# Wide moving operand in the convolutional stage, mLSTM decay rows on the free row half, and a reordered opening of the feed-forward stages

## The reference

```python
def swiglu(h, w_gu, w_down):                 # four times
    g, u = jnp.split(h @ w_gu, 2, axis=-1)
    return (jax.nn.silu(g) * u) @ w_down

# mLSTM scores of the mixer of the first stack, 8 heads of 64: exp(decay terms) * (q @ k.T)

def conv_gated_ffn(x, w_up, conv_w, conv_b, w_down):      # twice
    h = x @ w_up                              # 1024 -> 2 * 2816
    h = causal_depthwise_conv(h, conv_w, width=3) + conv_b
    gate, val = jnp.split(h, 2, axis=-1)
    return (jax.nn.silu(gate) * val) @ w_down
```

## Time and profile before

| | |
|---|---|
| time, three runs | 1957.45 us median (1957.35 to 1958.13) |
| the profiled execution | 1958.44 us, its span 1955.8 us |
| PE busy | 1941.7 us (99%), 11580 matmuls |
| PEld busy | 1706.1 us (87%) |
| DVE busy | 1269.5 us (65%) |
| ACT busy | 1099.4 us (56%) |
| DMA | 335.82 MB, mean 172 GB/s |

### The profile page before, as it was taken

How to read it: one execution, slowest core, us unless ns; L and a number is a source line. 1 busy time by engine, 2 the same in 40 slices (tenths; PEclk the granted TensorE clock), 3 DMA queues, 4 the chain that set the end, 5 groups by cost and what they waited for, 6 DMA issues and landing times.

```text
span 1955.8 us, 29401 instructions
## 1 busy us (share of the span) xinstructions
PE 1941.7 (99%) x11580; PEld 1706.1 (87%) x11580; DVE 1269.5 (65%) x2141; ACT 1099.4 (56%) x1717; POOL 6.5 (0%) x18
## 2 busy tenths in 40 slices
PE   9999999999999999999999999999999999999998
PEld 7888899999788888888989988888989998989997
DVE  5555777466655575557865676556758777758775
ACT  5444666554644564456774655446656556646554
POOL 0000000000000000000000000000000000000000
PEclk9999999999999999999999999999999999999999
DMA  8656445546566556645454546664536555536562
GB/s 278 192 184 184 161 132 171 162 131 197 187 190 186 172 184 193 185 156 175 134 179 152 155 158 217 188 184 146 166 108 205 181 186 165 160 114 199 179 187 82
DMA packets 93688, 335.82 MB, mean 172 GB/s; under 512 B 10224, under 2 KB 12528, under 8 KB 93552
## 3 DMA queue, kind: packets, MB, share of 16 engines
q1 hardware_dynamic: 92112, 328.51, 54.0%
q0 software_dynamic: 720, 4.37, 0.6%
q10 hardware_dynamic: 720, 1.07, 0.2%
HBM read 332.86 MB, written 1.05 MB: 171 GB/s over the span
## 4 chain that ended last, share of the span: by engine, by line
PE 94%; DVE 4%; ACT 1%; DMA 1%; issue 1%; DVEq 0%; ACTq 0%
PE stream L1797 11%; PE stream L1798 10%; PE stream L1799 10%; PE stream L1803 10%; PE stream L1805 10%; PE stream L1804 10%; PE acc L1803 8%; PE acc L1805 8%; PE acc L1804 8%; PE stream L1897 1%; DVE w_lo L1061 1%; PE acc L2208 1%; PE acc L2006 1%; DMA w_raw<-in_w_down 1%; PE stream L2203 0%
## 5 line engine op out<-in xcount | busy, mean ns | idle before, releaser
L1061 DVE TENSOR_TENSOR w_lo<-w_raw,w_hi 128x1024 fp32r<-128x1024 f32 x624 | 759.7, 1223 | 391.4 <-ACT w_hi L550 390.4
L550 ACT ACTIVATE w_hi<-w_raw 128x1024 fp32r<-128x1024 f32 x624 | 655.1, 1055 | 423.4 <-PE stream L1805 208.6
L1797 PE MATMUL stream<-h_hi,w_hi 128*128 128x256 f32 x1440 | 417.0, 290 | 1.1 <-DVE conv_tiles L1513 0.9
L1798 PE MATMUL stream<-h_lo,w_hi 128*128 128x256 f32 x1440 | 407.0, 283 | 0.0
L1799 PE MATMUL stream<-h_hi,w_lo 128*128 128x256 f32 x1440 | 407.0, 283 | 0.0
L1803 PE MATMUL stream<-w_hi,h_hi 128*128 128x512 f32 x896 | 353.9, 395 | 0.0
L1805 PE MATMUL stream<-w_lo,h_hi 128*128 128x512 f32 x896 | 349.2, 390 | 0.0
L1804 PE MATMUL stream<-w_hi,h_lo 128*128 128x512 f32 x896 | 348.8, 389 | 0.0
L1797 PEld LDWEIGHTS stream<-h_hi,w_hi 128*128 128x128 f32 x1440 | 275.4, 191 | 6.4 <-issue 2.4
L1798 PEld LDWEIGHTS stream<-h_lo,w_hi 128*128 128x128 f32 x1440 | 275.7, 191 | 0.9
L1799 PEld LDWEIGHTS stream<-h_hi,w_lo 128*128 128x128 f32 x1440 | 275.3, 191 | 0.0
(11 more groups left out here) (312 smaller groups left out, 2183.3 us busy)
## 6 DMA issues: line engine op xcount, KB each, us to landing
w_raw<-in_w_up SPq DMA_DIRECT2D x264, 512.0 KB, 3.7
w_raw<-in_w_mix SPq DMA_DIRECT2D x228, 512.0 KB, 3.6
w_raw<-in_w_down SPq DMA_DIRECT2D x132, 512.0 KB, 3.7
params<-in_params POOLq DMA_DIRECT2D x4, 859.5 KB, 5.7
out_x<-x_residual SPq DMA_DIRECT2D x4, 256.0 KB, 2.4
constants<-in_consts POOLq DMA_DIRECT2D x1, 832.0 KB, 7.6
x_residual<-in_x ACTq DMA_DIRECT2D x3, 256.0 KB, 7.1
x_residual<-in_x SPq DMA_DIRECT2D x1, 256.0 KB, 3.6
```

Source lines behind the costliest of these rows:

```text
L550: nc.scalar.activation(w_hi[:, u % RING], w_raw[:, u % RAW], ACT.Copy).then_inc(hi_ready, 1)
L1061: nc.vector.tensor_tensor(w_lo[:, u % RING], w_raw[:, u % RAW], w_hi[:, u % RING].bitcast(F32), ALU.subtract).then_inc(split_done, 1)
L1797: nc.tensor.matmul(dst, w_hi[:, s, w], hi, start=first, stop=False)
L1798: nc.tensor.matmul(dst, w_hi[:, s, w], lo, start=False, stop=False)
```

## The change

- The convolutional stage: h_hi and h_lo become two halves of one tile h_both. A k-block is now one matmul with 512 moving columns, [h_hi | h_lo], against w_hi, and one with 256 columns, h_hi, against w_lo. A bank then holds two partial sums side by side. For i > 1 ACT copies the second half to a new tile c_sum (semaphore conv_part), DVE adds the first half to it (semaphore conv_in), and the convolution reads c_sum. PE takes a bank again when the sum of i-2 is made, not when its convolution is done (i = 3 is as before).
- The mLSTM scores: the decay rows and the row selector also lie in partitions 64 to 127; a head reads them from the half that its q and k do not use, and the five matmuls alternate.
- The opening of `ffn`: one of the five splits ahead of the root moves behind the rounding of chunk 0, on ACT and on DVE.

```diff
         mo_tok, _ = sb("out_gate_tok", [P, QT, D], at=h32_at)
-        h_hi, _ = sb("h_hi", [P, KT, T], F32R)
-        h_lo, _ = sb("h_lo", [P, KT, T], F32R)
+        h_both, _ = sb("h_both", [P, KT, 2 * T], F32R)
+        h_hi, h_lo = h_both[:, :, 0:T], h_both[:, :, T:2 * T]
         cst, _ = sb("constants", [P, NC])
...
-        sel_r, _ = sb("row_select", [64, HEADS], F32R)
+        sel_r, _ = sb("row_select", [P, HEADS], F32R)
...
-        nm, _ = sb("neg_m_rows", [64, T], F32R)
+        nm, _ = sb("neg_m_rows", [P, T], F32R)
...
+        c_sum, _ = sb("conv_sums", [P, 4, T])
...
         def conv_tile(i, side_i):
-            return (side[side_i] if i == 0 else bank[2 * (i % 2) + side_i])[:, 0:T]
+            return (side[side_i] if i == 0 else bank[2 * (i % 2) + side_i])[:]
+
+        def conv_src(i, side_i):
+            return conv_tile(i, side_i)[:, 0:T] if i < 2 else c_sum[:, 2 * (i % 2) + side_i]
 
...
 
-                for j in range(5):
+                for j in range(4):
                     hi_next()
...
                 chunk_round(0)
+                hi_next()
                 hi_next()
...
                     for side_i in range(2):
+                        if i > 1:
+                            act.wait_ge(unit_done, u0 + up2_at(i, side_i) + 1)
+                            act.wait_ge(conv2_done, 2 * n + side_i - 3)
+                            nc.scalar.activation(c_sum[:, 2 * (i % 2) + side_i], conv_tile(i, side_i)[:, T:2 * T],
+                                                 ACT.Copy).then_inc(conv_part, 1)
                         if 2 * i + side_i >= 3:
...
                         else:
-                            act.wait_ge(unit_done, u0 + up2_at(i, side_i) + 1)
+                            act.wait_ge(conv_in, 2 * (l * (NF - 2) + i - 2) + side_i + 1)
                         if n > 1:
                             act.wait_ge(gated, n - 1)
-                        nc.scalar.activation(cbuf[:, 2 * (i % 2) + side_i], conv_tile(i, side_i), ACT.Identity,
+                        nc.scalar.activation(cbuf[:, 2 * (i % 2) + side_i], conv_src(i, side_i), ACT.Identity,
                                              scale=p2("conv_w", (2 * 2 + side_i) * NF + i),
...
 
-                for j in range(5):
+                for j in range(4):
                     lo_next()
...
                 chunk_rest(0)
+                lo_next()
                 lo_next()
...
                                                     ALU.mult)
-                        nc.vector.tensor_tensor(sel_r[:], ident[0:64, 0:HEADS], ident[0:64, 32:32 + HEADS],
-                                                ALU.add)
+                        for b in (0, 64):
+                            nc.vector.tensor_tensor(sel_r[b:b + 64], ident[b:b + 64, b:b + HEADS],
+                                                    ident[b:b + 64, b + 32:b + 32 + HEADS], ALU.add)
                     nc.vector.tensor_tensor(lamp[:, 0:1], p1("lam", 0), p1("lam", 1), ALU.mult)
...
                     dve.wait_ge(nm_cleared, l + 1)
-                    nc.vector.tensor_copy(nm[0:HEADS], neg_m[:]).then_inc(rows_split, 1)
-                    dve.wait_ge(rows_split, l * 2 + 1)
-                    nc.vector.tensor_tensor(nm[32:32 + HEADS], neg_m[:], nm[0:HEADS].bitcast(F32),
-                                            ALU.subtract).then_inc(rows_split, 1)
+                    for b in (0, 64):
+                        nc.vector.tensor_copy(nm[b:b + HEADS], neg_m[:]).then_inc(rows_split, 1)
+                    dve.wait_ge(rows_split, l * 4 + 2)
+                    for b in (32, 96):
+                        nc.vector.tensor_tensor(nm[b:b + HEADS], neg_m[:], nm[0:HEADS].bitcast(F32),
+                                                ALU.subtract).then_inc(rows_split, 1)
 
...
                         s = 2 * (i % 2) + side_i
+                        if i > 1:
+                            dve.wait_ge(conv_part, 2 * (l * (NF - 2) + i - 2) + side_i + 1)
+                            nc.vector.tensor_tensor(c_sum[:, s], conv_tile(i, side_i)[:, 0:T], c_sum[:, s],
+                                                    ALU.add).then_inc(conv_in, 1)
                         if 2 * i + side_i >= 3:
...
                             r = nc.vector.scalar_tensor_tensor(
-                                out=cbuf[:, s, back:], in0=conv_tile(i, side_i)[:, 0:T - back],
+                                out=cbuf[:, s, back:], in0=conv_src(i, side_i)[:, 0:T - back],
                                 scalar=p2("conv_w", ((2 - back) * 2 + side_i) * NF + i),
...
                         pe.wait_ge(qk_silu, l + 1)
-                        pe.wait_ge(rows_split, l * 2 + 2)
+                        pe.wait_ge(rows_split, l * 4 + 4)
                         pe.wait_ge(sc_masked, (n8 + HEADS) * 2)
...
                     q, k = y[r, h // 2], y[r, 4 + h // 2]
-                    row = sel_r[:, h:h + 1].to_broadcast([64, P])
+                    z = slice(64 - 64 * (h % 2), 128 - 64 * (h % 2))
+                    row = sel_r[z, h:h + 1].to_broadcast([64, P])
                     nc.tensor.matmul(side[1][:, 0:3 * P], ident_r[:], neg_r[:], start=True, stop=False)
-                    nc.tensor.matmul(side[1][:, 0:T], row, nm[:], start=False, stop=False)
-                    nc.tensor.matmul(side[1][:, T:3 * P], row, nm[:, P:T], start=False,
-                                     stop=True).then_inc(mlstm_sc, 1)
                     nc.tensor.matmul(side[0][:, 0:T], k[:, 0:P], q, start=True, stop=True)
+                    nc.tensor.matmul(side[1][:, 0:T], row, nm[z], start=False, stop=False)
                     nc.tensor.matmul(side[0][:, T:3 * P], k[:, P:T], q[:, P:T], start=True,
                                      stop=True).then_inc(mlstm_qk, 1)
+                    nc.tensor.matmul(side[1][:, T:3 * P], row, nm[z, P:T], start=False,
+                                     stop=True).then_inc(mlstm_sc, 1)
 
...
                             pe.wait_ge(open_taken, l * 2 + side_i + 1)
+                        elif i == 3:
+                            pe.wait_ge(conv2_done, 2 * (l * NF + i - 2) + side_i + 1)
                         else:
-                            pe.wait_ge(conv2_done, 2 * (l * NF + i - 2) + side_i + 1)
-                        model_unit(conv_tile(i, side_i), u, h_hi, h_lo,
-                                   (lambda k: turn_open(1) if k == 4 else None) if (i, side_i) == (2, 0) else None)
+                            pe.wait_ge(conv_in, 2 * (l * (NF - 2) + i - 4) + side_i + 1)
+                        dst = conv_tile(i, side_i)
+                        for k in range(KT):
+                            if k == 4 and (i, side_i) == (2, 0):
+                                turn_open(1)
+                            w = slice(k * P, (k + 1) * P)
+                            nc.tensor.matmul(dst, w_hi[:, u % RING, w], h_both[:, k], start=(k == 0), stop=False)
+                            r = nc.tensor.matmul(dst[:, 0:T], w_lo[:, u % RING, w], h_hi[:, k], start=False,
+                                                 stop=(k == KT - 1))
+                        r.then_inc(unit_done, 1)
                     if i >= LAG:
```

More of the change, by code:

```diff
@@ L390, in build @@
         ln_stat = sem("ln_stat")
+        conv_in = sem("conv_in")
+        conv_part = sem("conv_part")
         open_out = sem("open_out")
```

## The result

The changed kernel takes 1947.81 us (median of 5 runs, 1947.64 to 1948.49) against 1957.45 us of the kernel before (5 runs, 1957.24 to 1958.69): 9.6 us less, a ratio of 0.995 with a 95% interval of 0.9939 to 0.9961. 1946.0 was predicted. In the profiled executions the span goes from 1955.8 to 1946.0 us, 9.8 less.

The account below looks back on a forecast made before the run. PE was taken to bound the kernel, with 94% of the chain. Convolutional part 6.0 + mLSTM scores 3.4 + opening 2.0 = 11.4 us less than 1957.45 us gave 1946 us; forecast range 1943 to 1950 us, chance 0.62.

Parts of the forecast that it names:

- Convolutional steps: Convolutional stage: a k-block falls from 359.4 to 348.8 ns, 10.6 ns on each of 640, saving 6.8 us.
- I take the steps as they stand: Convolutional k-block: a wide step of 229 ns and a narrow one of 119.8 ns, as profiled before, make 348.8 ns.
- rival A: The convolutional part gives nothing, for instance with wide steps near 240 ns: 1952 us; chance 0.16.
- The estimate by the page: Convolutional stage: with the page's fixed 2.5 ns a matmul, dropping 640 matmuls would be worth only 1.6 us.
- i = 3: Convolutional stage: PE waits longer for the convolution of i = 1, costing 0.35 us over two layers.
- End of the stage: End of the convolutional stage: a longer ACT and DVE chain makes PE wait 0.2 us a layer, 0.4 us in all.
- ACT and DVE in the turn: Convolutional turn: ACT busy 5.47 us and DVE 7.06, against PE's 8.33; neither becomes the bound by its work.
- Rival C: DVE becomes the bound of the convolutional turn, 9.0 us in place of 8.33: 1970 us; chance 0.05.
- Rival B: More gain: wide convolutional steps of 226.5 ns and no end wait, 13.8 us saved, under 1943 us; chance 0.08.
- mLSTM scores: mLSTM scores: every head takes 1.02 us, even heads saving 0.33 and odd ones 0.10, 3.4 us in all.
- In the new order only one decay matmul stands among the passes: mLSTM head: that one decay matmul is shorter than q·k's, so q·k alone sets the length, 1.02 us.
- Opening: Opening: waits of 1.12 and 1.09 us before chunk 0's turning go in stages 1 and 3, less 0.2: 2.0 us.

Follow-up runs that it names:

- conv_no_sum: The changed kernel without ACT's copy and DVE's addition of each bank's second half; 1948.70 us, ratio 0.9951 to the kernel before.
- wide_first: The changed kernel with each convolutional up unit's eight wide matmuls first, then its eight narrow ones; 1944.87 us, ratio 0.9935 to the kernel before.
- conv_only: The kernel before with the convolutional part of the change alone; 1953.05 us, ratio 0.9978 to the kernel before.
- early_turn: The changed kernel with the opening's second turning ahead of k = 2, not k = 4, of the unit of i = 2; 1946.22 us, ratio 0.9944 to the kernel before.
- m_no_decay: The changed kernel without the decay matmuls in the mLSTM scores; 1948.17 us, ratio 0.9948 to the kernel before.
- m_qk_first: The changed kernel with a head's mLSTM matmuls ordered mask, both q·k, both decay rows; 1948.30 us, ratio 0.9949 to the kernel before.

## Why the prediction was right, and where its terms were off

The time is 1.8 us above the forecast and inside the range, and every part saves time where it was said to. But the terms were mis-sized in both directions, and the number came out closer than they did. The two larger terms were 1.7 and some 1.6 us too high; the opening brought 0.5 to 0.8 us more than its term for a reason that was not foreseen, and all three together 0.6 to 1.1 us more than the parts alone. That this brought the sum near is luck. One of the prediction's own signs of being wrong also came: the wide steps against h_both are longer than those of the down units, 236 against 229 ns.

- **Convolutional steps**, 6.8 us at 10.6 ns a k-block. The step "I take the steps as they stand", 229 and 119.8 ns as they stand apart in the down and up units, is what failed. Where the two widths alternate a k-block is 352.5 ns, 6.9 ns less than before. A full turn is 8.387 us against 8.500, 0.113 and not 0.17 us less; over 36 turns that is 4.1 us. A down unit with a change of width at each end did not show what alternation at every step does. conv_no_sum and wide_first put it on the order of PE's matmuls; why that order is slower stays open. It is the condition of rival A in part, at 236 ns where A names 240.
- **The estimate by the page.** The Trainium skill, page "TensorE: Matmul & The Clock Gate", section "Wait — 56ns, not 53.3ns?", gives a fixed 2.5 ns for a matmul, from which the prediction estimated 1.6 us for the 640 matmuls. The turns give 4.1 us and conv_only 4.3; the trace does not agree.
- **i = 3**, -0.35 us: the stop went from 0.9 to 1.2 us, as said. early_turn shows what it hangs on.
- **End of the stage**, -0.2 us a layer: 0.17 us in the first, and gone in conv_no_sum. In the second layer PE's steps show no such stop, so the two layers cost 0.17 and not 0.4 us.
- **ACT and DVE in the turn**, 5.47 and 7.06 us: 5.32 and 6.87. PE stops for neither inside these turns. Rival C did not come. (Rival B's 13.8 us would give 1943.7, not under 1943; nothing hangs on it.)
- **mLSTM scores**, 3.4 us at 1.02 us a head. "In the new order only one decay matmul stands among the passes" was a wrong reading: the gap was put down to the decay matmuls since they stood near it. Every head is 1.11 us, and the part is worth 1.9 us, near its lower bound of 1.8; m_no_decay shows that a head without decay rows is as long. So the free half was the right cause for the even heads, and the further 0.10 us a head had a wrong one.
- **Opening**, 2.0 us; measured 2.5 to 2.8. Both stops of 1 us went, stage 0's stayed, as said. The 0.2 us of new wait in stage 0 did not come, and 0.3 us in each of stages 1 and 3 was missed, since a stop of 0.2 us stands in no list of waits.

The sum by the parts alone, 4.3 + 1.7 + 2.5 = 8.5 us by medians or 9.2 by spans, is under the 9.6 and 9.8 of all three. Part of the difference is in stops of 0.2 us that some executions have and others not, and 0.2 us is the slower pattern of steps that conv_only has at i = 3 and 4 of its second layer; what of it is more than that stays open.

## What to carry to other kernels

A step that is read where two kinds of instruction stand apart need not hold where they alternate; time the pattern that the kernel will have, and try blocks of two. A wait at a place in a list can hide a second one just behind it, so follow the chain one consumer further, and look at the steps themselves. Before a gap is put down to the instructions beside it, take those out: it costs one run.

## What the runs showed of the hardware that was not expected

- Alternating matmuls of 512 and 256 columns have two stable patterns, 347 and 353 ns a pair, in one kernel at one granted clock (1.00 in the window above). In the eight turns it is always the slower. Two and two take 347.7, eight and eight 347.5. What selects the pattern stays open: after the same full stop both are seen, the faster one in 4 layers and the slower in 10.
- Matmuls on different row halves do not keep the order of the program. In m_qk_first the last matmul of the head starts at 368.60, the second pass of the head's second one at 368.69. The Trainium skill, page "TensorE: Matmul & The Clock Gate", section "The mechanism", has matmuls start and end in the order of the program; the trace does not agree for starts where one of the two takes two passes.
- Going from 128 rows to 64 costs 0.10 us and then another 0.11 in the first pass: the mask of 384 columns is 0.160 us at 2.4 GHz, q·k starts 0.26 us behind it, and its weight load starts with it. On the way back the first matmul's step is 0.10 us longer too. Both places also change between fp32r and plain fp32, and no run parts the two; but `carry`, plain fp32 on all 128 rows, has its load 0.22 us ahead of its matmul (1486.20 and 1486.42), so a load that starts this late goes with the rows. The Trainium skill, page "TensorEngine Tiling (Array Packing)", section "Key Properties", says that a change of the tiling mode drains the engine; the trace agrees, in that no weight load of the head's 64-row matmuls starts before the mask's 0.160 us are over.
